# Loading and converting the first block of a one-core layer kernel in single k tiles

## The reference

```
def rms_norm(x, w):
    xf = x.astype(jnp.float32)
    y = xf * lax.rsqrt(jnp.mean(xf * xf, axis=-1, keepdims=True) + NORM_EPS)
    return (y * w.astype(jnp.float32)).astype(x.dtype)
...
    for layer in range(DEPTH):
        h = rms_norm(x, attn_norm_w[layer])
        proj = h @ w_in[layer]
        hq, hf, hi, hg, c_q, c_kv, k_r = jnp.split(proj, IN_SPLITS, axis=-1)
```

## Time and profile before

| | us |
|---|---|
| median of 3 runs (lowest to highest) | 1107.96 (1107.83 to 1108.14) |
| the profiled execution | 1108.18 |
| its span, first to last instruction | 1106.4 |
| PE busy | 1099.8 |
| DVE busy | 903.4 |
| ACT busy | 645.0 |
| POOL busy | 66.0 |

### The profile page before, as it was taken

The page is one execution under the profiler, slowest core; times in us unless marked ns, Lnnn a source line. Parts: engine busy times, 40 slices in busy tenths (PEclk is TensorE's granted clock), DMA queues, the critical chain, the costliest instruction groups (busy, mean ns, idle before and its releaser), DMA issues.

```text
span 1106.4 us, 15300 instructions
## 1 busy us (share of the span) xinstructions
PE 1099.8 (99%) x5154; PEld 926.2 (84%) x5154; DVE 903.4 (82%) x1250; ACT 645.0 (58%) x907; POOL 66.0 (6%) x164
## 2 busy tenths in 40 slices
PE   9999999999999999999999999999999999999998
PEld 9988888888888878888888888888888888888887
DVE  6688797587876587688888988988988889999887
ACT  6676766668654456365465455554554555654553
POOL 1500000000000010000100100001011010000000
PEclk9999999999999999999999999999999999999999
DMA  9866455454655486767777777777777777666655
GB/s 301 292 185 203 132 169 165 151 161 152 231 171 186 156 235 195 236 218 209 246 233 222 237 232 217 236 234 227 225 235 228 247 255 236 218 214 204 199 201 171
DMA packets 108083, 234.21 MB, mean 212 GB/s; under 512 B 8448, under 2 KB 17408, under 8 KB 107776
## 3 DMA queue, kind: packets, MB, share of 16 engines
q1 hardware_dynamic: 101360, 211.34, 59.1%
q0 software_dynamic: 6528, 22.03, 6.9%
q10 hardware_dynamic: 144, 0.20, 0.1%
HBM read 221.99 MB, written 11.53 MB: 211 GB/s over the span
## 4 chain that ended last, share of the span: by engine, by line
PE 97%; DVE 1%; ACT 1%; DMA 0%; issue 0%; SPq 0%; DVEq 0%; ACTq 0%
PE side L2036 24%; PE main L1802 21%; PE side L2038 12%; PE main L1805 11%; PE side L2006 4%; PE side L2008 4%; PE side L2007 4%; PE main L2006 3%; PE main L2008 3%; PE main L2007 3%; PE main L1822 1%; PE side L1928 1%; PE side L1844 0%; DMA raw<-in_w_in 0%; PE side L1879 0%; PE side L1880 0%
## 5 line engine op out<-in xcount | busy, mean ns | idle before, releaser
L1051 ACT CAST w_hi<-raw 128x1024 fp32r<-128x1024 f32 x245 | 239.7, 984 | 158.8 <-PE side L2036 85.4
L1640 DVE TENSOR_TENSOR w_lo<-raw,w_hi 128x1024 fp32r<-128x1024 f32 x245 | 274.2, 1131 | 13.9 <-ACT w_hi L1051 13.9
L1162 DVE TENSOR_TENSOR w_lo<-raw,w_hi 128x1024 fp32r<-128x1024 f32 (+3 forms) x156 | 178.7, 1155 | 94.4 <-ACT w_hi L829 93.1
L829 ACT CAST w_hi<-raw 128x1024 fp32r<-128x1024 f32 (+3 forms) x155 | 153.1, 996 | 127.1 <-PE main L1802 116.1
L1802 PE MATMUL main<-w_hi,hT_hi 128*128 128x512 f32 (+2 forms) x416 | 160.9, 388 | 0.0
L1805 PE MATMUL main<-w_hi,hT_lo 128*128 128x512 f32 (+2 forms) x416 | 157.6, 380 | 0.0
L2036 PE MATMUL side<-w_hi,hT_hi 128*128 128x512 f32 x400 | 155.6, 389 | 0.0
L2038 PE MATMUL side<-w_hi,hT_lo 128*128 128x512 f32 x400 | 155.6, 389 | 0.0
L1802 PE MATMUL main<-w_lo,hT_hi 128*128 128x512 f32 (+2 forms) x416 | 107.1, 379 | 0.0
L2036 PE MATMUL side<-w_lo,hT_hi 128*128 128x512 f32 x400 | 106.9, 389 | 0.0
L1805 PEld LDWEIGHTS main<-w_hi,hT_lo 128*128 128x128 f32 x416 | 78.2, 188 | 12.9
(11 more groups left out here) (308 smaller groups left out, 1890.1 us busy)
## 6 DMA issues: line engine op xcount, KB each, us to landing
raw<-in_w_gate_up SPq DMA_DIRECT2D x176, 512.0 KB, 4.7
raw<-in_w_down SPq DMA_DIRECT2D x88, 512.0 KB, 4.3
raw<-in_w_in SPq DMA_DIRECT2D x64, 512.0 KB, 4.3
raw<-in_w_out SPq DMA_DIRECT2D x32, 512.0 KB, 3.6
raw<-in_w_in SPq DMA_DIRECT2D x15, 384.0 KB, 5.5
squares<-hiddenT POOLq DMA_DIRECT2D x11, 512.0 KB, 4.5
hiddenT<-squares POOLq DMA_DIRECT2D x44, 128.0 KB, 5.4
raw<-in_w_ukv SPq DMA_DIRECT2D x8, 512.0 KB, 4.2
```

The lines of the kernel that those rows point to most:

```text
L829: copy(w_hi[:, slot, 0:n], raw[:, slot, 0:n]).then_inc(s_hi, 1)
L1051: copy(w_hi[:, n % RING, 0:cols], src).then_inc(s_hi, 1)
L1162: tt(w_lo[:, slot, 0:n], raw[:, slot, 0:n], w_hi[:, slot, 0:n].bitcast(F32), ALU.subtract)\
L1640: tt(w_lo[:, n % RING, 0:cols], src, w_hi[:, n % RING, 0:cols].bitcast(F32), ALU.subtract)\
```

## The change

The first ten k tiles are pieces of their own, so the first block has 13 granules in place of 9. Token piece p is asked for directly behind weight granule p. The positions of x's copy, the small inputs, the squares and the root move by the four added granules. The constant tile is multiplied 8 times in place of 14.

```diff
-PIECES = [(0, 1), (1, 1)] + [(k, 2) for k in range(2, KT, 2)]
+SINGLES = 10
+PIECES = [(k, 1) for k in range(SINGLES)] + [(k, 2) for k in range(SINGLES, KT, 2)]
...
-FILLERS = 14
-
-XT_AFTER = {1: (1,), 2: (2,), 3: (3, 4), 4: (5,), 5: (6,), 6: (7,), 7: (8,)}
-X_AFTER = {11: 0, 13: 1, 15: 2, 17: 3}
-SMALL_AFTER = 20
-
-X_SPLIT = (FIRST, FIRST + 1, -1, 0, 1, 2, 3, 4, 5)
+FILLERS = 8
+
+X_AFTER = {15: 0, 17: 1, 19: 2, 21: 3}
+SMALL_AFTER = 24
+
+X_SPLIT = (FIRST, FIRST + 1) + tuple(p - LEAD for p in range(2, len(PIECES)))
...
-    s = [(at, ("sq1", c)) for c, at in enumerate((12, 14, 16, 18))]
-    s += [(19, ("r1a",)), (20, ("r1b",))]
+    s = [(at, ("sq1", c)) for c, at in enumerate((16, 18, 20, 22))]
+    s += [(23, ("r1a",)), (24, ("r1b",))]
...
-                for p in XT_AFTER.get(g, ()):
-                    load_tokens(p)
+                if g < len(PIECES):
+                    load_tokens(g)
```

## The result

The changed kernel takes **1110.85 us** (15 runs, 1109.21 to 1111.53) against 1107.96 (15 runs, 1107.44 to 1108.39): ratio 1.0023, interval 1.0017 to 1.0030. I had forecast 1106.4 with 1105.4 to 1108.8. It is slower by 2.9 us by the medians.

What follows compares the result with a forecast made beforehand. The opening was taken as bound by the third k tile's arrival. A gain of 1.68 us, less some 0.1 at the switch to pairs, gave -1.6: 1107.96 to 1106.4, range 1105.4 to 1108.8.

Steps and rivals of the forecast that it cites:

- What bounds the kernel: PE is busy 1099.8 of 1106.4 us; only the opening can gain, bounded by the third k tile's arrival.
- the constant products: Opening: eight in place of 14 start the layer's products at 4.69, 1.69 us earlier; worth 0 by itself.
- The conversion: First block: ACT and DVE convert single tiles within PE's 1.04 us per tile; priced at 0, else 0.5 us.
- Arrival of tiles 2 and 3: Opening: the same bytes land at the same time, so tile 2 starts at 7.87; gain 1.68 us.
- rival (a): Opening: the third tile comes without its lag, about 3.1 us after issue; gain 2.2 to 2.5, 1105.6; chance 0.20.
- lower bound: Opening: tile 2's weights and tokens land as late as before; tiles start at 8.45, gain about 0.7.
- The load loop: First block: slots hold four tiles; last pair ends at 11.5 + 3L, no loss below L = 3.7; priced 0.
- L: First block: time from asking for a granule's load to its landing; 3.5 us by the prediction's map.
- Rival (b): First block: the load loop binds if L stays near 5.9 us, 1112.8; at 4.9, 1109.8; chance 0.17.
- Rival (c): Opening: the clock rises later, at 9.15; gain only 0.7, 1107.3; chance 0.06 with other small gains.
- 0.45 us for slow first products: Opening: the products from 4.69 run 0.9 us at half clock rate until 5.6, costing 0.45 us.
- The rule on request size: First block's loads: at least 1 MiB per DMA is advised, smaller requests lower the rate; at 294 GB/s, 1107.1.

Runs made afterwards that it cites:

- e1: The changed kernel with 14 constant products in place of 8: 1109.98 us against 1108.40 for the kernel before, ratio 1.0017.
- e2: The kernel before with 8 constant products in place of 14: 1108.51 us, ratio 1.0002.
- e11: The changed kernel with fourteen single tiles, one pair, and places of their own for raw weights of granules 4 to 11: 1107.31 us against 1107.95, ratio 0.9993.
- e12: The same kernel as e11, run again: 1107.65 us against 1108.46 for the kernel before, ratio 0.9992.
- e5: The changed kernel run once more, unaltered: 1110.81 us against 1108.02 for the kernel before, ratio 1.0021.
- e9: The kernel before with each two-tile request of the first block made as two one-tile requests: 1108.16 us against 1107.95, ratio 1.0001.
- e6: The changed kernel with six single tiles in place of ten, then five pairs: 1109.63 us, ratio 1.0013 to the kernel before.
- e10: The changed kernel with four more constant products on PE right ahead of granule 10: 1110.02 us against 1107.95 for the kernel before, ratio 1.0018.
- e8: The changed kernel with six single tiles, five pairs, and places of their own for raw weights of granules 4 to 11: 1107.98 us against 1108.02, ratio 1.0003.

## Why the prediction was wrong

**What bounds the kernel, and the constant products**: right. What the change did, it did in the opening, and e1 and e2 show no effect of the constant products by themselves. The start came at 4.56 (4.69 forecast). That PE has one large wait behind the opening held for the trace I had; four of the thirteen later ones have another near 900 us. The conversion, priced at 0, kept up (e11, e12).

**Arrival of tiles 2 and 3**: "I assume that the same bytes land at the same time" was too cautious at first: tile 2 started at 7.13, not 7.87, and the idle stretch of 0.65 ahead of it did not come. That was the sign of rival (a), whose gain came only up to there. Then the assumption was too kind. From 8 to 16 us 294 GB/s came in place of 380, as fewer bytes were asked for at a time. (Its lower bound has a slip: if x2 lands at 8.27, ACT's 0.5 and 0.15 put the start at 8.92 and not 8.45, a gain of 0.5 and not 0.7. Nothing hangs on it.)

**The load loop**: this is the step that failed. "I take 0 for it", 0.5 kept in the text for the switch, and 0.1 of that in the sum; it measured 1.6 us there in one trace and 2.2 in the other, and 0.2 to 0.3 more in waits within the pairs. Three things went wrong in it. I followed the loop over granules 4, 8 and 12, while the one that binds goes 2, 6, 10. I took one L for singles and pairs, 3.5; they had 2.7 to 3.9 and 4.6. And I checked the last pair against the end of the block, not the first pair against a PE that is a whole pair ahead. In numbers 11.86 + 4.6 + 1.75 + 0.1 = 18.3, where my pace for PE (tile 2 ended at 9.14, seven more at 1.04) brings it there at 16.4.

**Rival (b)** was the right one, and it had 0.17. Of its signs, PE idle ahead of granule 10 came; landings of single requests over 4.3 us did not (2.7 to 3.9 in the first trace). Its numbers ran through three rounds of one L, which is not what happened, so that its middling case gives 1109.8, the median of the runs not at 0.998, is luck.

**Rival (c), the clock**: right in kind and misplaced. I looked for it at the start, where the products follow each other; it comes behind the largest idle stretch, 1.5 us by the medians of the two halves, and I gave (b) no clock of its own. As to my 0.45 us for slow first products: in e5 the first two start 0.39 us apart, in the first trace the first four 0.2 apart. The rows read a granted clock of 1.00 in both, and under the constant tile too, so the low level at the start is a reading of the durations alone.

**The rule on request size**: the Trainium skill, page "DMA: Bandwidth & Descriptors", section "Rules for kernel authors", asks for large requests. e9 agrees in direction (340 against 380 GB/s, not told apart from SP's doubled number of requests) and shows that the kernel before had room for it.

**The range** ended at 1108.8 and left out even the fastest of the 26 runs of the change (1109.05), which is not at 0.998: it is missed without the low clock already, and the clock adds to that. "Slower" had 0.07.

**Left open**: the first trace is 0.6 us late at the end of the first block and 1.0 at its end; 0.3 of that arises near 58 us, where PE reaches the first transposes of the latents. e6's trace has the same and the other traces don't; what made it was not tried. e5's is 2.96 late at the end of the block and 3.3 at its end. That every run at 0.998 has its fall behind the stall is concluded from e5's trace and from e10's 11 runs. Why the stall varies from run to run is not known, and the changed kernel with its tokens asked for earlier was not run.

## What to carry to other kernels

Loads cut to half their size halve the bytes in flight when the number of slots stays as it is: work out the loop (landing, conversion, next request) for the slot that the first large request uses, with a landing time for its own size, and compare it with PE's arrival there. A lead won by small pieces was paid back at the switch to large ones in every kernel that kept its four slots. What kept it here were places of their own with a late switch (e12); with an early one they were not enough (e8). And an idle stretch of PE of 2 us may cost nearly as much again behind it, as in e5; price it with and without the lower clock.

## What the runs showed that I had not expected

The clock fell to 1.2 GHz at 20.06, after PE had been back at work since 19.18, and stayed there for 3.4 us of unbroken work. The same kernel with an idle stretch of 1.45 us in its trace did not show it, and the one in which 1.05 of 1.23 us were filled has no run of 11 at 0.998. And busy DMA engines did not mean the highest rate: their busy share in 8 to 16 us was 0.95 at 294 GB/s in the changed kernel and 1.04 at 380 in the old one.
